# An encoder trunk whose MLP weight blocks are summed: one block sum made by an accumulating transfer

## The reference

```python
def sq_relu_mlp(y, w_up, w_down):      # w_up 1024 x 4096, w_down 4096 x 1024
    u = y @ w_up
    return jnp.square(jax.nn.relu(u)) @ w_down

for i in range(DEPTH):
    y = rmsnorm(h, norm_gains[i, 0])
    y = mlstm_mixer(...) if i % 2 == 0 else diff_attention(...)
    h = h + y
    h = h + sq_relu_mlp(rmsnorm(h, norm_gains[i, 1]), mlp_w_up[i], mlp_w_down[i])
h = rmsnorm(h, final_gain)
```

## Time and profile before

| | |
|---|---|
| median of 3 runs | 1187.46 us (1187.4 to 1188.97) |
| the profiled execution | 1187.75 us |
| its span, first to last instruction | 1185.8 us |
| TensorE busy, matmul | 1171.1 us, 99% |
| VectorE busy | 975.4 us, 82% |
| ScalarE busy | 791.7 us, 67% |
| POOL busy | 115.9 us, 10% |
| granted TensorE clock | 0.998 of full |
| moved by DMA | 131.76 MB, 111 GB/s |

### The profile page before, as it was taken

How to read it: one execution, slowest core, us unless ns; L and a number is a source line. 1 busy time by engine, 2 the same in 40 slices (tenths; PEclk the granted TensorE clock), 3 DMA queues, 4 the chain that set the end, 5 groups by cost and what they waited for, 6 DMA issues and landing times.

```text
span 1185.8 us, 23197 instructions
## 1 busy us (share of the span) xinstructions
PE 1171.1 (99%) x8881; PEld 1124.6 (95%) x8881; DVE 975.4 (82%) x1487; ACT 791.7 (67%) x1401; POOL 115.9 (10%) x169
## 2 busy tenths in 40 slices
PE   9999999999999999999999999999999999999998
PEld 8999999999999999999999999987788999999987
DVE  6889888778988888885578989887889888898764
ACT  6777877746667666666357887787476675766753
POOL 3221120000010110112020000000001101001000
PEclk9999999999999999999999999999999999999999
DMA  7343332324382563574132122213335636546622
GB/s 180 96 105 93 89 101 86 99 84 145 95 189 77 135 151 107 121 197 151 54 92 70 54 71 71 88 37 93 121 113 136 143 107 154 132 122 145 190 78 72
DMA packets 152344, 131.76 MB, mean 111 GB/s; under 512 B 23176, under 2 KB 143040, under 8 KB 152256
## 3 DMA queue, kind: packets, MB, share of 16 engines
q1 hardware_dynamic: 141600, 104.93, 30.3%
q0 software_dynamic: 10528, 25.52, 9.5%
q10 hardware_dynamic: 128, 0.09, 0.0%
HBM read 111.37 MB, written 19.17 MB: 110 GB/s over the span
## 4 chain that ended last, share of the span: by engine, by line
PE 71%; issue 18%; DVE 7%; ACT 2%; POOL 1%; DMA 1%; SPq 0%; DVEq 0%; POOLq 0%; ACTq 0%
PE ps L2408 33%; PE ps L2125 18%; PE ps L2360 12%; PE ps L2627 2%; PE ps L2180 1%; DVE lof L1709 1%; DVE lo L1723 1%; PE ps L2198 1%; DVE lo L1716 1%; ACT hi L780 1%; DVE blocks_f L1763 1%; DMA xin<-in_x_dram 1%; DVE ps L1741 1%; PE ps L2312 0%; PE ps L2266 0%
## 5 line engine op out<-in xcount | busy, mean ns | idle before, releaser
L780 ACT ACTIVATE hi<-lof 128x1024 fp32r<-128x1024 f32 x92 | 95.1, 1054 | 105.5 <-DVE lof L1709 105.5
L2125 PE MATMUL ps<-yh,wh 128*128 128x264 f32 (+1 forms) x704 | 160.6, 302 | 0.0
L2125 PE MATMUL ps<-yl,wh 128*128 128x264 f32 (+1 forms) x704 | 155.3, 295 | 0.0
L2125 PE MATMUL ps<-yh,wl 128*128 128x264 f32 (+1 forms) x704 | 155.3, 295 | 0.0
L1716 DVE TENSOR_TENSOR lo<-lof,hi 128x1024 fp32r<-128x1024 f32 x92 | 111.2, 1222 | 49.5 <-ACT hi L780 49.5
L780 ACT ACTIVATE hi<-raw 128x1024 fp32r<-128x1024 f32 (+1 forms) x128 | 111.3, 894 | 37.0 <-PE ps L2360 20.0
L2408 PE MATMUL ps<-th,hi 128*128 128x264 f32 (+1 forms) x448 | 126.7, 283 | 0.0
L2408 PE MATMUL ps<-th,lo 128*128 128x264 f32 (+1 forms) x448 | 126.5, 282 | 0.0
L2408 PE MATMUL ps<-tl,hi 128*128 128x264 f32 (+1 forms) x448 | 126.5, 282 | 0.0
L2408 PE MATMUL ps<-yh,hi 128*128 128x264 f32 (+1 forms) x408 | 116.0, 284 | 1.4 <-DVE lo L1716 1.4
L2408 PE MATMUL ps<-yl,hi 128*128 128x264 f32 (+1 forms) x408 | 116.1, 285 | 0.7 <-DVE lo L1723 0.7
(11 more groups left out here) (331 smaller groups left out, 3465.6 us busy)
## 6 DMA issues: line engine op xcount, KB each, us to landing
raw<-in_mlp_w_up_dram SPq DMA_DIRECT2D x32, 1024.0 KB, 6.4
raw<-in_mlp_w_down_dram SPq DMA_DIRECT2D x32, 1024.0 KB, 5.0
raw<-in_diff_w_in_dram SPq DMA_DIRECT2D x24, 512.0 KB, 3.7
raw<-in_mlstm_w_in_dram SPq DMA_DIRECT2D x16, 512.0 KB, 4.5
h_sum<-abuf POOLq DMA_DIRECT2D x24, 264.0 KB, 7.6
h_sum<-abuf POOLq DMA_DIRECT2D x24, 256.0 KB, 7.0
raw<-in_mlstm_w_in_dram SPq DMA_DIRECT2D x16, 256.0 KB, 5.2
raw<-in_mlstm_w_out_dram SPq DMA_DIRECT2D x3, 1024.0 KB, 4.9
```

Source lines behind the costliest of these rows:

```text
L780: return nc.scalar.activation(o, i, ACT.Copy, scale=scale)
L2125: last = mm(ps[:, bank + s, 0:w_], w[:, slot, kb, :], m[:, kb, t0:t0 + w_], start=(kb == 0 and n == 0), stop=(kb == CB - 1 and n == 2))
```

## The change

For a crossed pair, POOL adds A22 from HBM onto the A21 quarter of `raw` with an accumulating transfer (`weight_sum`, 46 of them, 256 KB each in rows of 512 bytes) once the load has landed; `raw` then holds S1 where A21 was. S1 and A22 are now split together straight from `raw` by one copy and one subtraction of eight row blocks (`natural_hi(i, 1)`, `natural_lo(i, 1)`), waiting for `m_sum`, and S4 is split alone (four row blocks). Three forms remain: S2 = S1 - A11, S3 = A22 - S2, S4 = A12 - S2. The groups are A1, S1A22, S23, S4; SP's next load waits for S1A22. In POOL's queue the sums stand between the stores and sends. The split of S4(i+1) and the plain pair's second split stand ahead of the second part of `block_forms`. `refine_factor` runs at pair 0 ahead of `forms_lo`, with `acc` as scratch, and `scale_residual` waits for `ln_done`. Two pairs of semaphores are merged or dropped (`gates_sent`, `ms_rd`). The diff, cut:

```diff
-READY = counted((i, e) for i in range(PAIRS) for e in (("A1", "S14", "S23", "A22") if crossed(i) else (0, 1)))
+READY = counted((i, e) for i in range(PAIRS) for e in (("A1", "S1A22", "S23", "S4") if crossed(i) else (0, 1)))
-SLOT = {"A11": 0, "A12": 1, "S2": 2, "S3": 3, "S1": 4, "S4": 5, "A22": 6}
+SLOT = {"S2": 2, "S3": 3, "S4": 4}
+NATURAL = {"A11": (0, 0), "A12": (0, 1), "S1": (20, 0), "A22": (20, 1)}
+GROUP = {"A11": "A1", "S1": "S1A22", "A22": "S1A22", "S2": "S23", "S4": "S4"}
...
+        def raw_landed(layer, i):
+            return m_raw[i % 2], 16 * (PAIRS // 2 * layer + i // 2 + 1)
+        def raw_summed(layer, i):
+            crosses = [k for k in range(i % 2, PAIRS, 2) if crossed(k)]
+            return m_sum[i % 2], 16 * (len(crosses) * layer + crosses.index(i) + 1)
...
-                        sp.wait_ge(m_lo, layer * N_READY + READY[i - 2, "A22" if crossed(i - 2) else 1])
+                        sp.wait_ge(m_lo, layer * N_READY + READY[i - 2, "S1A22" if crossed(i - 2) else 1])
...
+                def weight_sum(i):
+                    g, c0 = i // 8, 256 * (i % 4) + P
+                    a22 = columns(up, g * D + c0, P) if is_up(i) else down[g, :, :, c0:c0 + P]
+                    pool.wait_ge(*raw_landed(layer, i))
+                    pool.dma_start(raw[:, i % 2, first_k(i), P:2 * P], a22[:, second_k(i), :],
+                                   accum_op=ALU.add).then_inc(m_sum[i % 2], 16)
+                def send_sum(i, m):
+                    pool.wait_ge(m_out, N_OUT * layer + SENT_OUT[i, m])
+                    pool.dma_start(h_sum[2 * (i % 8) - 8 + m, :, t0:T], ab[m][:, t0:T], accum_op=ALU.add).then_inc(h_sent[m], 16)
                 for q in range(4):
-                    pool.wait_ge(h_scaled, FACTOR * layer + q + 1)
+                    if q % 2 == 0:
+                        weight_sum(PLAIN + q // 2)
+                    pool.wait_ge(h_scaled, FACTOR * layer + q + 3)
...
-                for i in range(PAIRS):
-                    for m in range(2):
-                        if not sent_down(i):
-                            continue
-                        pool.wait_ge(m_out, N_OUT * layer + SENT_OUT[i, m])
-                        pool.dma_start(h_sum[2 * (i % 8) - 8 + m, :, t0:T], ab[m][:, t0:T], accum_op=ALU.add).then_inc(h_sent[m], 16)
+                for i in range(PAIRS - 7):
+                    if sent_down(i - 1):
+                        send_sum(i - 1, 1)
+                    if i + 3 > PLAIN + 1 and crossed(i + 3):
+                        weight_sum(i + 3)
+                    if sent_down(i):
+                        send_sum(i, 0)
...
+                def natural_hi(i, m):
+                    act.wait_ge(*(raw_summed if m else raw_landed)(layer, i))
+                    act.wait_ge(m_done, items + last_use(i, "A22" if m else "A12"))
+                    copy(hi[1 - i % 2][:, slots(i, m), :], raw[:, i % 2, :, P * m:P * m + P]).then_inc(m_hi, 1)
...
-                            form_hi(i + 1, "S14")
+                            natural_hi(i + 1, 1)
...
-                        natural_hi(i + 1, False)
+                        form_hi(i + 1, "S4")
...
+                    x, y = {"S2": (s1, a11), "S3": (a22, f[:, 8:12, :]), "S4": (a12, f[:, 8:12, :])}[name]
+                    if name == "S2":
+                        dve.wait_ge(*raw_summed(layer, i))
...
                         plain_lo(layer, 1, 1)
+                        refine_factor()
                         for n in range(4):
                             forms_lo(n)
...
                     if crossed(i + 1):
-                        form_lo(i + 1, "S14")
+                        natural_lo(i + 1, 1)
...
+                    if crossed(i + 1):
+                        form_lo(i + 1, "S4")
+                    elif 1 <= i < PAIRS - 1:
+                        plain_lo(layer, i + 1, 1)
                     if i < PAIRS - 8 and i % 8 == 3:
                         block_forms(i, ("S3", "S1", "S2", "A22"), 1)
-                    if crossed(i + 1):
-                        natural_lo(i + 1, False)
-                    elif 1 <= i < PAIRS - 1:
-                        plain_lo(layer, i + 1, 1)
...
-                    if i == PLAIN:
-                        refine_factor()
-                    elif not is_up(i) and not in_tail(layer, i) and not sent_down(i):
+                    if not is_up(i) and not in_tail(layer, i) and not sent_down(i):
                         evacuate(i, 0)
                     if crossed(i + 2):
                         if not (sent_down(i) and i % 8 == DOWN_FROM - 1):
-                            natural_lo(i + 2, True)
-                        form(i + 2, "S1", 0)
-                        form(i + 2, "S3", 0)
-                        form(i + 2, "S2", 1)
-                        form(i + 2, "S4", 3)
+                            natural_lo(i + 2, 0)
+                        form(i + 2, "S2", 0)
+                        form(i + 2, "S3", 1)
+                        form(i + 2, "S4", 1)
...
-                        group = {"A11": "A1", "S2": "S23", "S1": "S14", "A22": "A22"}[name]
-                        pe.wait_ge(m_lo, ready + READY[i, group])
+                        pe.wait_ge(m_lo, ready + READY[i, GROUP[name]])
```

More of the change, by code:

```diff
@@ L397, in program @@
         m_raw = [sem(f"m_raw{i}") for i in range(RAW)]
+        m_sum = [sem(f"m_sum{i}") for i in range(RAW)]
         m_hi, m_lo, s_made, m_done, c_done, m_evac, m_out = sems("m_hi m_lo s_made m_done c_done m_evac m_out")
@@ L509, in last_use @@
                 return DONE[p, item]
-            return DONE[p, 1 if item in ("S4", "A22") else 0]
+            return DONE[p, 1 if item == "A22" else 0]
         def last_plain_use(i, m):
@@ L998, in plain_hi @@
             def plain_hi(layer, i, m):
-                act.wait_ge(m_raw[i % 2], 16 * (PAIRS // 2 * layer + i // 2 + 1))
+                act.wait_ge(*raw_landed(layer, i))
                 if i >= 2:
@@ L1034, in form_hi @@
                 def form_hi(i, group):
-                    act.wait_ge(s_made, 4 * (ranks + RANK[i] - 1) + (3 if group == "S23" else 4))
+                    act.wait_ge(s_made, 3 * (ranks + RANK[i] - 1) + (2 if group == "S23" else 3))
                     act.wait_ge(m_done, items + last_use(i, "S3" if group == "S23" else "S4"))
-                    rows = slice(8, 16) if group == "S23" else slice(16, 24)
+                    rows = slice(8, 16) if group == "S23" else slice(16, 20)
                     copy(hi[1 - i % 2][:, rows, :], lof[1 - i % 2][:, rows, :]).then_inc(m_hi, 1)
-                def natural_hi(i, both):
-                    act.wait_ge(m_raw[i % 2], 16 * (PAIRS // 2 * layer + i // 2 + 1))
-                    act.wait_ge(m_done, items + last_use(i, "A12" if both else "A22"))
-                    if both:
-                        copy(hi[1 - i % 2][:, 0:8, :], raw[:, i % 2, :, 0:P]).then_inc(m_hi, 1)
-                    else:
-                        copy(hi[1 - i % 2][:, 24:28, :], raw[:, i % 2, second_k(i), P:2 * P]).then_inc(m_hi, 1)
+                def natural_hi(i, m):
+                    act.wait_ge(*(raw_summed if m else raw_landed)(layer, i))
+                    act.wait_ge(m_done, items + last_use(i, "A22" if m else "A12"))
+                    copy(hi[1 - i % 2][:, slots(i, m), :], raw[:, i % 2, :, P * m:P * m + P]).then_inc(m_hi, 1)
                 def snap(i, what):
@@ L1714, in form_lo, with natural_lo @@
                     dve.wait_ge(m_hi, layer * N_READY + READY[i, group])
-                    rows = slice(8, 16) if group == "S23" else slice(16, 24)
+                    rows = slice(8, 16) if group == "S23" else slice(16, 20)
                     V.tensor_tensor(lo[1 - i % 2][:, rows, :], lof[1 - i % 2][:, rows, :],
                                     hi[1 - i % 2][:, rows, :].bitcast(F32), ALU.subtract).then_inc(m_lo, 1)
-                def natural_lo(i, both):
-                    dve.wait_ge(m_hi, layer * N_READY + READY[i, "A1" if both else "A22"])
-                    rows, src = (slice(0, 8), raw[:, i % 2, :, 0:P]) if both else (slice(24, 28), raw[:, i % 2, second_k(i), P:2 * P])
-                    V.tensor_tensor(lo[1 - i % 2][:, rows, :], src, hi[1 - i % 2][:, rows, :].bitcast(F32),
-                                    ALU.subtract).then_inc(m_lo, 1)
+                def natural_lo(i, m):
+                    dve.wait_ge(m_hi, layer * N_READY + READY[i, "S1A22" if m else "A1"])
+                    V.tensor_tensor(lo[1 - i % 2][:, slots(i, m), :], raw[:, i % 2, :, P * m:P * m + P],
+                                    hi[1 - i % 2][:, slots(i, m), :].bitcast(F32), ALU.subtract).then_inc(m_lo, 1)
@@ L1773, in scale_residual @@
                 def scale_residual(q):
-                    dve.wait_ge(ms_rd, layer + 1)
+                    dve.wait_ge(ln_done, norm + 1)
                     rows = h[:, 2 * q:2 * q + 2, t_in:T]
@@ L2391, in product @@
```

(7 more changed lines are left out.)

46 lines of the change are left out of this document (22 added, 24 removed).

## The result

The changed kernel takes 1228.9 us (median of 4 runs, 1227.1 to 1233.8) against 1187.6 us before (4 runs beside it, 1187.4 to 1189.0): the ratio is 1.035, 95% interval 1.034 to 1.037. The prediction was 1182.9 us, with a range up to 1194.0. The profiled execution took 1227.1 us, with a span of 1225.4 us where before had 1185.8: 39.6 us more.

The account below looks back on a forecast made before the run. TensorE, busy 1171.1 of 1185.8 us, was taken as the bound, leaving only its MLP waits to gain. Terms 2.1 + 1.7 + 1.1 + 0.5 = 5.4, less 0.8, gave 4.6: 1187.46 - 4.6 = 1182.9 us, range 1180.8 to 1194.

Parts of the forecast that it names:

- kinds B, C and D: TensorE's MLP waits: pair 5's snapshot (gain 1.7 us), pair 6's snapshot (0.5), S1 split of last down pairs (2.1).
- the 6.7: Ceiling in us of any gain in the MLPs: 5.0 of idle time plus 1.7 of pipeline refill.
- my ten waits: TensorE's waits inside the MLPs before the change: four in layer 0 (2.0 us), six in layer 1 (3.0 us).
- Part 1 and 2: One sum form fewer per pair on VectorE (31.5 us); S1 and A22 split at transfer landing, gaining 2.1 and 1.7 us.
- Part 3: Pair 4's split moved ahead of the second four block forms: 1.9 us, less 0.8 for late activations, leaving 1.1.
- wait A: TensorE's wait for pair 4's low split, one per layer, 0.7 and 0.9 us idle; forecast to go.
- Parts 4 and 5: Norm factor's two steps moved to the start, and S4's split counted separately after C1; each forecast to cost nothing.
- Part 6: 46 new POOL transfers of 256 KB: 0.9 us issue, 4.7 us landing, 0.8 us lost in all.
- 120 ns a piece: Cost per 512-byte sum piece (3.9 us per sum) from which delayed residual transfers were said to begin costing time.
- 2 us of room: Slack claimed at a down group's end between ScalarE's snapshot and TensorE's need for it at 427.5.
- the 0.8 that I took for everything: Loss in us over six places at down group ends, allowed for variation of landings.
- Slower: Rival, chance 0.20: sums hold up residual transfers, TensorE loses 2.8 us at six places, 16.8 in all; 1199.6 us.

Follow-up runs that it names:

- the moves alone: Kernel before with only the early norm factor and, in pairs 3 and 11, the next weight tile's split ahead of the second block sums: 1187.8 us, ratio 1.0001.
- The order without bytes: Regrouped kernel with the fourth form added on VectorE, plus GpSimd waiting for each load where the sums would stand, no transfers: 1188.0 us.
- sums of 2 columns: Changed kernel with each weight sum cut to 2 of its 128 columns, pieces of 8 bytes, same order and piece count: 1205.2 us.
- the run with 64 columns: Changed kernel with each weight sum cut to 64 of its 128 columns, same order and piece count: 1216.9 us.

## Why the prediction was wrong, point by point

- **What bounds the kernel, and the ceiling.** Right in the main. The waits of kinds B, C and D vanish in the change, and the regrouped kernel without transfers gains 6.3 us. That this is so near the 6.7 is partly luck: that kernel still loses some 2.1 us at two waits for `al`, so 1.7 us of its gain lay outside my ten waits, and the 6.7 was no true ceiling.
- **Part 1 and 2** (regrouping). Right for B and D; the reason was half right. I let the freed form of 684 ns help; the run with that form kept on VectorE shows that it isn't needed.
- **Part 3** (wait A). Too high. The term was 1.1 us after taking back 0.8; the moves alone gave nothing, since `al` took the place of the split with 1.5 us. In the change itself, with VectorE 26.7 us lighter, 0.3 us remain there, so its saved form does count at this one place.
- **Parts 4 and 5.** Nothing in the traces speaks against a cost of nothing.
- **Part 6** (the transfers) is the step that failed, and in it the landings of the load and the send, 6.4 and 5.1 us. The sizes of the sum itself were well taken: it lands after 4.8 us in the median (4.7), a piece takes 57 to 72 ns (56), an issue on GpSimd 1.30 us, of which 0.76 pass before the next (0.9). The rule that I built on them was wrong: that the hold-up begins to cost only from 120 ns a piece. I took the load from the median of all loads, let the send land 5.1 us after its issue, near the 4.2 us of one that was alone at first, and added them as if they did not meet. In the change the load takes 8.9 us and the send behind it another 8.9 at the place that I had worked out: 6.3 us more against 2 us of room, and TensorE lost 3.9 us there (437.62 - 433.58, less the pace of 0.12). The order without bytes costs 6.7 us already, against the 0.8 that I took for everything.
- The trace of before had these two times at that very place, with the load of pair 17 and the send of pair 14 in flight together (DMA issues from 417.2 to 417.3):

```profile
raw<-in_mlp_w_up_dram SPq DMA_DIRECT2D x1, 1024.0 KB, 7.5
h_sum<-abuf POOLq DMA_DIRECT2D x1, 264.0 KB, 8.0
```

With them my own sum gives 412.2 + 7.5 + 0.9 + 8.0 = 428.6 for the landing of the send, behind the 427.5 at which TensorE wants the snapshot, with no dear piece at all.
- I followed one send behind one sum. The queue holds two sends behind each, and ScalarE, VectorE and SP are all in the loop behind them; the next load starts late as well. I priced six places with a fixed delay each, and none of what a delay does to the next pair.
- **The clock** was not in the sum at all. A wait of TensorE was priced as its idle time and 0.17 us. For a stall of some 4 us, that leaves out the matmuls behind it at half clock.
- **The rivals.** *Slower* named the place, the queue and the signs: TensorE waits on `pu`, behind `abuf` that waits for `h_sum`. It had the wrong trigger (dear pieces and issues over 2 us, neither of which came, and sums landing after 9 us, which one of 46 did, at 517.73) and a price of 16.8 us where 47.7 were lost. I gave it 0.20 and cut my range inside it. The row that should have moved both stood in my own text: a sum that waits for a load, ahead of transfers that a reader waits for, in a queue that is in order. I asked how long the sum takes, when the question was how long the queue stands still and what goes out at once when it moves.
- The rule of the Trainium skill on ring order (the same section as above), by which a send waits for the pieces of the sum ahead of it, goes the right way: 32 pieces of 23 to 38 ns are 0.8 to 1.2 us, and the sends land 1.5 us later with sums of 2 columns than with none (6.0 against 4.5). Its 2.0 us plus bytes at 436 GB/s (same page, Anatomy of one DMA), an estimate of 2.6 us for a sum, does not: 4.8 us measured.

## What to carry to other kernels

Before a wait goes into an in-order issue queue, ask what stands behind it, who waits for that, and what will be issued together when the wait ends; put work that is already due ahead of it. A landing time read from a trace holds only for the traffic that it met there: take it from the place where the transfers will meet, not from a lone one or a median, and add the turn that the delay makes through the loop. Ask also how early the load goes out that the queue will wait for. When a change mixes a new resource with a new grouping, try the grouping without the resource first: here it held all of the gain.

## What the runs showed of the hardware

- A piece of an accumulating transfer from HBM costs 23 to 38 ns with 8 bytes, 43 to 58 ns with 256 (16.5% of 1215.1 us in the run with 64 columns) and 57 to 72 ns with 512 in the transfer engines, by whether the share of the kernel with the order alone or of the kernel before is taken off. Halving the bytes does not halve the time.
- An accumulating issue with 512 rows takes GpSimd 1.30 us, and the next instruction starts 0.76 us after it; with 128 rows it takes 0.89.
- The granted clock of TensorE in the 4 us behind a stall was 0.50 to 0.54 after four idle times of 3.75 to 5.72 us, 0.64 after one of 3.67 us, 0.59 after one of 2.67 us, and 0.60 and 1.00 after two of 1.81 us; behind waits up to 1.2 us it stayed at 1.00.
